# Two transformer blocks on one core: bias tables by a single fp32 product, and another order of the first loads

## What is computed

```python
h = rmsnorm(x, norm_mix[0])
b_gate, c_gate, u = jnp.split(h @ w_in, 3, axis=-1)
```

```python
bucket = t5_bucket(k_pos[None, :] - q_pos[:, None])
bias = rel_bias[bucket].astype(jnp.float32).transpose(2, 0, 1)
s = jnp.einsum('bhcqd,bhcsd->bhcqs', qblk, kt).astype(jnp.float32) * scale + bias[None, :, None]
```

## Time and profile before

| what | value |
|---|---|
| median of 3 runs | 1266.78 us (1266.71 to 1266.91) |
| the profiled execution | 1267.27 us |
| its span | 1265.4 us |
| TensorE busy | 1239.2 us, 98% of the span |
| VectorE, ScalarE, POOL busy | 79%, 67%, 3% |
| instructions | 18129 |
| DMA, moved in all | 325.22 MB, mean 257 GB/s |

### The profile page before, as it was taken

One profiled execution on the slowest core, in us unless ns is written; L12 is line 12 of the kernel. 1 busy time (PEld: TensorE's weight loads), 2 busy tenths in 40 slices (PEclk: granted clock), 3 DMA queues, 4 the chain that ended last, 5 costly groups with the idle time before them and its releaser, 6 DMA issues.

```text
span 1265.4 us, 18129 instructions
## 1 busy us (share of the span) xinstructions
PE 1239.2 (98%) x5924; PEld 1017.3 (80%) x5924; DVE 1001.6 (79%) x1397; ACT 844.1 (67%) x1218; POOL 39.1 (3%) x47
## 2 busy tenths in 40 slices
PE   7999999999999999999999999999999999999998
PEld 6888888888778787888788888888786877888887
DVE  6577555556977899999999999999999887765664
ACT  5666444446755788888888878888887587544442
POOL 0000000000100000000000000000100121000000
PEclk9999999999999999999999999999999999999999
DMA  9735555554233699999999999999996633455540
GB/s 356 275 133 215 190 193 175 190 199 166 68 133 134 252 379 373 378 348 365 368 379 360 353 360 379 375 356 366 376 422 264 238 146 115 163 176 195 178 155 34
DMA packets 48197, 325.22 MB, mean 257 GB/s; under 512 B 5417, under 2 KB 6705, under 8 KB 9873
## 3 DMA queue, kind: packets, MB, share of 16 engines
q1 hardware_dynamic: 44704, 316.40, 66.3%
q10 hardware_dynamic: 2752, 5.77, 1.2%
q0 software_dynamic: 688, 2.36, 0.5%
HBM read 318.74 MB, written 5.77 MB: 256 GB/s over the span
## 4 chain that ended last, share of the span: by engine, by line
PE 91%; DVE 4%; ACT 2%; issue 1%; DMA 0%; POOL 0%; SPq 0%; DVEq 0%; ACTq 0%
PE bank L431 26%; PE bank L433 25%; PE bank L432 25%; PE bank L1138 4%; PE bank L1139 2%; PE bank L495 2%; PE bank L845 1%; ACT wh L1196 1%; DVE wl L1827 1%; PE bank L467 1%; PE bank L700 1%; PE bank L1137 1%; PE bank L699 1%; DMA x<-x_dram 0%; DVE xt L1847 0%
## 5 line engine op out<-in xcount | busy, mean ns | idle before, releaser
L1827 DVE TENSOR_TENSOR wl<-raw,wh 128x1024 fp32r<-128x1024 f32 x598 | 714.7, 1219 | 178.0 <-ACT wh L1196 168.9
L1196 ACT ACTIVATE wh<-raw 128x1024 fp32r<-128x1024 f32 x598 | 630.6, 1058 | 273.1 <-PE bank L433 234.2
L431 PE MATMUL bank<-wh,xt 128*128 128x512 f32 (+2 forms) x1026 | 407.5, 397 | 5.7 <-DVE xt L1847 2.5
L433 PE MATMUL bank<-wh,xt 128*128 128x512 f32 (+2 forms) x1026 | 398.1, 388 | 0.0
L432 PE MATMUL bank<-wl,xt 128*128 128x512 f32 (+2 forms) x1026 | 397.5, 387 | 0.0
L431 PEld LDWEIGHTS bank<-wh,xt 128*128 128x128 f32 x1026 | 193.8, 189 | 44.3 <-DVE xt L1847 3.2
L433 PEld LDWEIGHTS bank<-wh,xt 128*128 128x128 f32 x1026 | 193.5, 189 | 40.6
L432 PEld LDWEIGHTS bank<-wl,xt 128*128 128x128 f32 x1026 | 194.1, 189 | 36.3
L431 PE MATMUL bank<-wh,hth 128*128 128x512 f32 x472 | 186.0, 394 | 1.1 <-DVE htl L1895 0.4
L433 PE MATMUL bank<-wh,htl 128*128 128x512 f32 x472 | 184.2, 390 | 0.0
L432 PE MATMUL bank<-wl,hth 128*128 128x512 f32 x472 | 183.8, 389 | 0.0
(11 more groups left out here) (304 smaller groups left out, 815.3 us busy)
## 6 DMA issues: line engine op xcount, KB each, us to landing
raw<-weights_dram SPq DMA_DIRECT2D x299, 1024.0 KB, 5.0
expert_results<-wide ACTq DMA_DIRECT2D x7, 512.0 KB
x<-x_dram SPq DMA_DIRECT2D x2, 512.0 KB, 7.7
wide<-bias_scratch ACTq DMA_DIRECT2D x8, 128.0 KB, 6.8
out_dram<-x SPq DMA_DIRECT2D x4, 256.0 KB, 2.0
fixed<-fixed_dram SPq DMA_DIRECT2D x1, 536.0 KB, 11.7
bias_scratch<-act ACTq DMA_DIRECT2D x2, 256.0 KB, 8.4
bias_scratch<-hbuf ACTq DMA_DIRECT2D x2, 256.0 KB, 15.1
```

Source lines behind the costliest of these rows:

```text
L431: mm(o, lh, wh[:, wi, sl], start=start, stop=False)
L433: return mm(o, ll, wh[:, wi, sl], start=False, stop=stop)
L1196: A(wh[:, c % SPLIT, 0:n], raw[:, (c // 2) % RAW, (c % 2) * UNIT:(c % 2) * UNIT + n], ACT.Copy).then_inc(hi_done, 1)
L1827: V.tensor_tensor(wl[:, c % SPLIT, 0:n], raw[:, (c // 2) % RAW, (c % 2) * UNIT:(c % 2) * UNIT + n], f32(wh[:, c % SPLIT, 0:n]), ALU.subtra ...
```

## The change

The four tables' eight products, two casts, one subtraction and four copies give way to one fp32 product with the bucket table (32 x 4) as its stationary side and the one-hot matrix as its moving side. It writes four rows of 512. It stands behind the third unit of the first chunk. One copy takes the four rows out, and one store on ScalarE's queue writes each of them 128 times.

The identity moves from `fixed` to the head of `cols`. SP's first loads become: columns with identity, first half of x, unit 0, second half of x, unit 1, panel 1, then the bucket table, the one-hot matrix, panel 2, `fixed`, and panels 3 to 5. POOL's two loads wait for unit 1.

```diff
         @block.sync
+            sp.dma_start(cols[:, :], cols_in).then_inc(sem("cols_in"), 16)
+            sp.dma_start(x[:, :, 0:WIDE], halves[:, :, 0:WIDE]).then_inc(sem("x_in0"), 16)
+            sp.dma_start(raw[:, 0, 0:UNIT], weights[0][:, 0:UNIT]).then_inc(sem("first_in"), 16)
+            sp.dma_start(x[:, :, WIDE:D], halves[:, :, WIDE:D]).then_inc(sem("x_in1"), 16)
+            sp.dma_start(raw[:, 0, UNIT:2 * UNIT], weights[0][:, UNIT:2 * UNIT]).then_inc(raw_full[0], 16)
+            sp.dma_start(raw[:, 1, :], weights[1]).then_inc(raw_full[1], 16)
             sp.dma_start(relb[:, :], relb_in).then_inc(sem("rel_in"), 16)
             sp.dma_start(onehot, onehot_in).then_inc(sem("rel_in"), 16)
-            sp.dma_start(fixed[:, 0:P], fixed_in[:, 0:P]).then_inc(sem("cols_in"), 16)
-            sp.dma_start(cols[:, :], cols_in).then_inc(sem("cols_in"), 16)
-            sp.dma_start(x[:, :, 0:WIDE], halves[:, :, 0:WIDE]).then_inc(sem("x_in0"), 16)
-            sp.dma_start(raw[:, 0, :], weights[0]).then_inc(raw_full[0], 16)
-            sp.dma_start(x[:, :, WIDE:D], halves[:, :, WIDE:D]).then_inc(sem("x_in1"), 16)
-            sp.dma_start(raw[:, 1, :], weights[1]).then_inc(raw_full[1], 16)
-            sp.dma_start(fixed[:, P:NFIXED], fixed_in[:, P:NFIXED]).then_inc(sem("fixed_in"), 16)
-            for p in range(2, RAW):
+            sp.dma_start(raw[:, 2, :], weights[2]).then_inc(raw_full[2], 16)
+            sp.dma_start(fixed[:, :], fixed_in).then_inc(sem("fixed_in"), 16)
+            for p in range(3, RAW):
...
         @block.gpsimd
+            g.memset(half[:, :], -0.5).then_inc(sem("half"), 1)
+            pool.wait_ge(sem("half"), 1)
+            pool.wait_ge(raw_full[0], 16)
             pool.dma_start(rows[:, :], rows_in.to_broadcast((P, NROWS))).then_inc(sem("pos_in"), 16)
             pool.dma_start(posi[:, :], pos_in).then_inc(sem("pos_in"), 16)
...
         @block.tensor
-            rel_bias(0)
-            rel_bias(1)
-            pe.wait_ge(sem("cols_in"), 32)
+            def rel_bias():
+
+                pe.wait_ge(sem("rel_in"), 32)
+                mm(bank[4][0:NB2, :], relb[:, :], onehot, start=True, stop=True).then_inc(sem("rel_T"), 1)
+
+            pe.wait_ge(sem("cols_in"), 16)
             turn_half("mix0", 0, 4)
-            rel_bias(2)
-            rel_bias(3)
             turn_half("mix0", 1, 6)
...
-                chunk512(U_IN + 4 * j, 0, bank[2 * (j % 3):2 * (j % 3) + 2], normed("mix0") if j == 0 else None)
+                chunk512(U_IN + 4 * j, 0, bank[2 * (j % 3):2 * (j % 3) + 2], normed("mix0") if j == 0 else None,
+                         {2: rel_bias} if j == 0 else {})
...
         @block.scalar
-            for h in range(NB2):
-                sc.wait_ge(sem("rel_c"), h + 1)
-                sc.dma_start(scratch[h * P:(h + 1) * P, :], rel_rows[h]).then_inc(sem("rel_st"), 16)
+            sc.wait_ge(sem("rel_c"), 1)
+            sc.dma_start(scratch[0:NB2 * P, :].rearrange("(h p) n -> h p n", p=P),
+                         rel_rows[:, None, :].to_broadcast((NB2, P, WIDE))).then_inc(sem("rel_st"), 16)
...
             for c in range(4, SPLIT):
                 split_lo(c, 0)
+            dv.wait_ge(sem("rel_T"), 1)
+            V.tensor_copy(rel_rows, bank[4][0:NB2, :]).then_inc(sem("rel_c"), 1)
```

More of the change, by code:

```diff
@@ L90 @@
 _at = 0
-for _name, _n in (("mix0", 8), ("ffn0", 8), ("mix1", 8), ("ffn1", 8), ("attn2", 8), ("mlp2", 8), ("qa", 3), ("kva", 2),
+for _name, _n in (("ident", P), ("mix0", 8), ("ffn0", 8), ("mix1", 8), ("ffn1", 8), ("attn2", 8), ("mlp2", 8), ("qa", 3), ("kva", 2),
                   ("qn", 1), ("kn", 1), ("conv", 24), ("bq", 1), ("bk", 1), ("sub", 1), ("router", 64)):
@@ L105 @@
 _at = 0
-for _name, _n in (("ident", 128), ("mask", 384), ("ctab", 128), ("stab", 128), ("freq", 32), ("iota", 8),
+for _name, _n in (("mask", 384), ("ctab", 128), ("stab", 128), ("freq", 32), ("iota", 8),
                   ("before", 128), ("slots", 128), ("every", 128), ("fold", 8)):
@@ L189, in build @@
         by_expert = results[0:(NE - 1) * P, :].rearrange("(e p) n -> e p n", p=P)
-        ident = fixed[:, FIXED["ident"]:FIXED["ident"] + P]
+        ident = cols[:, COLS["ident"]:COLS["ident"] + P]
         maskt = fixed[:, FIXED["mask"]:FIXED["mask"] + 384]
         onehot = ebuf[0:BUCKETS, 0, :]
-        picked = hth[0:BUCKETS, 0:2, :]
-        relh, rell = (v[0:BUCKETS, 2:4, :].rearrange("p a (h n) -> p (a h) n", h=2) for v in (hth, htl))
-        rel_rows = (act[:, 0, 3072:3584], act[:, 1, 3072:3584], hbuf[:, 0, :], hbuf[:, 1, :])
+        rel_rows = act[0:NB2, 0, 3072:3584]
         NORMS = ("mix0", "ffn0", "mix1", "ffn1", "attn2", "mlp2")
@@ L313, in _ @@
         def _(sp):
+            halves = x_in.rearrange("(t p) d -> p t d", p=P)
+            sp.dma_start(cols[:, :], cols_in).then_inc(sem("cols_in"), 16)
[4 more added lines that the diff above has]
+            sp.dma_start(raw[:, 1, :], weights[1]).then_inc(raw_full[1], 16)
             sp.dma_start(relb[:, :], relb_in).then_inc(sem("rel_in"), 16)
             sp.dma_start(onehot, onehot_in).then_inc(sem("rel_in"), 16)
-            sp.dma_start(fixed[:, 0:P], fixed_in[:, 0:P]).then_inc(sem("cols_in"), 16)
-            sp.dma_start(cols[:, :], cols_in).then_inc(sem("cols_in"), 16)
-            halves = x_in.rearrange("(t p) d -> p t d", p=P)
-            sp.dma_start(x[:, :, 0:WIDE], halves[:, :, 0:WIDE]).then_inc(sem("x_in0"), 16)
-            sp.dma_start(raw[:, 0, :], weights[0]).then_inc(raw_full[0], 16)
-            sp.dma_start(x[:, :, WIDE:D], halves[:, :, WIDE:D]).then_inc(sem("x_in1"), 16)
-            sp.dma_start(raw[:, 1, :], weights[1]).then_inc(raw_full[1], 16)
-            sp.dma_start(fixed[:, P:NFIXED], fixed_in[:, P:NFIXED]).then_inc(sem("fixed_in"), 16)
-            for p in range(2, RAW):
+            sp.dma_start(raw[:, 2, :], weights[2]).then_inc(raw_full[2], 16)
+            sp.dma_start(fixed[:, :], fixed_in).then_inc(sem("fixed_in"), 16)
+            for p in range(3, RAW):
                 sp.dma_start(raw[:, p, :], weights[p]).then_inc(raw_full[p], 16)
@@ L351, in _ @@
             g = nc.gpsimd
+            g.memset(half[:, :], -0.5).then_inc(sem("half"), 1)
+            pool.wait_ge(sem("half"), 1)
+            pool.wait_ge(raw_full[0], 16)
             pool.dma_start(rows[:, :], rows_in.to_broadcast((P, NROWS))).then_inc(sem("pos_in"), 16)
             pool.dma_start(posi[:, :], pos_in).then_inc(sem("pos_in"), 16)
-            g.memset(half[:, :], -0.5).then_inc(sem("half"), 1)
-            pool.wait_ge(sem("half"), 1)
             def rsqrt(tag, a, b, n):
@@ L620, in _ @@
             for j in range(6):
-                if j < 2:
-                    pe.wait_ge(sem("rel_c"), 2 * j + 2)
+                if j == 2:
+                    pe.wait_ge(sem("rel_c"), 1)
                 if j >= 3:
                     pe.wait_ge(sem("in_c"), 2 * (j - 2))
-                chunk512(U_IN + 4 * j, 0, bank[2 * (j % 3):2 * (j % 3) + 2], normed("mix0") if j == 0 else None)
+                chunk512(U_IN + 4 * j, 0, bank[2 * (j % 3):2 * (j % 3) + 2], normed("mix0") if j == 0 else None,
+                         {2: rel_bias} if j == 0 else {})
                 if j == 3:
@@ L1190, in split_hi @@
             def split_hi(c, i):
-                sc.wait_ge(raw_full[(c // 2) % RAW], 16 * (c // ROUND + 1) + 16 * i)
+                if isinstance(i, int) and c + ROUND * i == 0:
+                    sc.wait_ge(sem("first_in"), 16)
+                else:
+                    sc.wait_ge(raw_full[(c // 2) % RAW], 16 * (c // ROUND + 1) + 16 * i)
                 if c >= SPLIT:
@@ L1311, in _ @@
             A(stat[:, 0:1], half[:, 0:1], ACT.Copy)
-            sc.wait_ge(sem("cols_in"), 32)
+            sc.wait_ge(sem("cols_in"), 16)
             for c in range(4):
@@ L1623, in _ @@
             squares("attn2", 1)
-            sc.wait_ge(sem("rel_st"), 16 * NB2)
+            sc.wait_ge(sem("rel_st"), 16)
             for h in range(NB2):
@@ L1969, in rotate @@
                 link(V.tensor_tensor(upper, t3, t4, ALU.add))
[L1972 to L1985, removed]
+            dv.wait_ge(sem("cols_in"), 16)
             for c in range(4):
@@ L2099, in _ @@
             dv.wait_ge(sem("norm_rs"), nth("ffn0") + 1)
-            dv.wait_ge(sem("rel_st"), 16 * NB2)
+            dv.wait_ge(sem("rel_st"), 16)
             ffn("ff", U_FF1, FF1 // FG, 2, 4, FG, 2, 0, leave=leave_ff1)
@@ L2872 @@
     cols = np.concatenate([
-        column(w["norm_mix"][0]), column(w["norm_ffn"][0]), column(w["norm_mix"][1]), column(w["norm_ffn"][1]),
+        np.eye(P, dtype=np.float32), column(w["norm_mix"][0]), column(w["norm_ffn"][0]), column(w["norm_mix"][1]), column(w["norm_ffn"][1]),
         column(w["attn_norm_g_2"][0]), column(w["mlp_norm_g_2"][0]), column(w["mla_q_a_norm"][0]),
```

8 lines of the change are left out of this document (removed).

## The result

The changed kernel takes **1279.76 us** (median of 4 runs, 1278.07 to 1280.71) against 1266.85 us for the kernel before, timed beside it (4 runs, 1266.71 to 1268.15). The ratio is 1.0103 with a 95% interval of 1.0090 to 1.0116: 12.9 us slower. The profiled execution took 1279.76 us, span 1278.0.

The account below looks back on a forecast made before the run. TensorE, busy 98%, was taken as the bound. Unit 6 at 10.6 + 36 x 0.2268 + 2.1 + 1.1 + 9.22 = 31.2 us against 32.86, 1.7 us earlier, took 1266.78 to 1265.1 us; range 1263.5 to 1267.4.

Parts of the forecast that it names:

- Part 4: Product, copy, angles, sine, issue and split ahead of unit 6: 9.22 us against 8.17 covered, TensorE waits 1.05 us.
- Part 5: Position load, fixed tables and table store cost nothing; positions land at 18.7 us, fixed tables near 18.
- The fourth rival: Four-partition table store, at an assumed sixteenth of 405 GB/s, clogs weight loads from 22.9 us: 1272 us; chance 0.04.
- Part 1: First loads reordered: x's halves land at 5.65 and 8.25 us, products start at 10.6 us, 4.0 earlier.
- Part 2: TensorE's low clock at the start of the products costs 2.1 us, against 1.9 before.
- Part 3: The one new fp32 product, behind unit 2 on TensorE's path, takes 1.1 us.
- the first rival: Angles' chain hides within units 3 to 5, the 1.05 us wait goes: 1263.4 to 1264.1 us; chance 0.24.
- The third rival: Position load lands late, at 26.7 us, and VectorE's wait delays unit 6: 1269.0 us; chance 0.06.

Follow-up runs that it names:

- e1: Changed kernel with the small zero-row store issued ahead of the table store on ScalarE's queue; 1266.71 us, ratio 0.9999 to the kernel before.
- e3: Changed kernel with the table store's source spread over all 128 partitions, each storing its row four times; 1264.84 us, ratio 0.9994 to the kernel before.
- e2: Changed kernel with the table store cut into four, one row from one partition each; 1273.22 us, ratio 1.0041 to the kernel before.
- e4: As e1, but with the load order of the kernel before the change; 1268.66 us, ratio 1.0015 to the kernel before.
- e5: As e3, with the copy behind the angle tables and the store behind the splits of units 6 to 9; 1266.55 us, ratio 1.0001.
- e7: Changed kernel with half the table store at its place, the other half behind the third group of units' splits; 1267.18 us, ratio 0.9999.
- e8: Changed kernel with the four source rows on partitions 0, 4, 8, 12; 1272.60 us, ratio 1.0046 to the kernel before.
- e9: Changed kernel with the four source rows on partitions 0, 32, 64, 96; 1275.97 us, ratio 1.0073 to the kernel before.
- e6: Changed kernel with the table store as two half-width stores, same bytes in twice the packets; 1292.13 us, ratio 1.0202 to the kernel before.

## Why the prediction was wrong

The forecast was 1265.1 us, no change. The sign came from one line.

**The step that failed** is in Part 4, "the sine, one DMA issue and the high part of unit 6", with the issue taken at 1.28 us as in the earlier trace rows, together with Part 5, which put the table store "at no cost". Part 5 asked of the store only when its data would be wanted, at 112.60 us. It did not ask what stands behind the store on its own queue. The next issue there was in the sum, at a price measured behind another store: before, the tables went out in four stores and the issue behind them took 1.28. Behind one store with 128 packets on each of four engines it measured 12.68. e1 takes that and nothing else away and the loss goes; e3 does the same by spreading the source.

**The fourth rival** had the store, the sign and roughly the size (1272), but another mechanism. In the changed kernel the weights were not clogged: from 27 to 32 us they still moved 1.79 MB. When unit 6 was wanted its weights were long in place, and only the engine that splits them stood still. The mechanism that the rival describes exists, and e2 shows it; it takes all 16 engines on one partition at a time, not four on four. Its assumed "sixteenth of 405 GB/s", 25, is what was measured.

**Part 1, the loads: right in kind, smaller.** The first transposes start at 5.19 (forecast 5.5 to 6.2), the products at about 11.2 (second product 11.63 less one slow pitch of 0.43; forecast 10.6). The second half of x was late: 7.2 us after its issue, near 9.4, where 8.25 was forecast. e4 puts the load order at 2.4 us, where 4.0 of earlier start less 0.2 for the clock had been forecast.

**Part 2, the clock: the price moves.** In the changed kernel the pitch fell near 13.5 us, 2.3 after the products began: 2.3 x 0.47 = 1.1 us lost for the 2.1 forecast. In e1, the same instructions up to there, it fell near 15.3, 3.9 after the start (second product 11.81 less 0.43), as it did before (3.84): 1.8 us. In e1's timeline the step is this:

```profile
14.80 0.63 PE L433 MATMUL bank<-wh,xt 128*128 128x512 f32 x1
15.23 0.53 PE L431 MATMUL bank<-wh,xt 128*128 128x512 f32 x1
15.60 0.39 PE L432 MATMUL bank<-wl,xt 128*128 128x512 f32 x1
15.82 0.39 PE L433 MATMUL bank<-wh,xt 128*128 128x512 f32 x1
```

**Part 3, the product: right.** Two instructions, 20.61 to 21.55, 0.94 us for 1.1. The four passes of the Trainium skill ("FP8 and Floating Point Precision", TensorE Precision Notes) gave an estimated 0.85; the row lies between.

**Part 4, the rest of the chain: right.** With an issue of 1.28 in place of 12.68 unit 6 would have been ready at 42.00 - 11.40 = 30.6 us (forecast 31.2), and e3 measures the wait as 0.61 (forecast 1.05). In e1, with the zero row's issue out of the chain, TensorE doesn't wait at all: the first rival, "the chain hides", has the mechanism right as soon as that one issue is elsewhere, though not its time (1263.4 to 1264.1, where e1 took 1266.71).

**Part 5, the landings: right.** The positions landed at about 12.1 + 6.9 = 19.0 us (forecast 18.7), the fixed tables at 5.8 + 12.5 = 18.3 (forecast 18), and VectorE's cast at 22.27 waited for neither. The third rival falls.

Without the hold the forecast would have held: e1, e3, e5 and e7 measure 0.9994 to 1.0001, all with intervals that take in no change. None of them beats the kernel before by what can be measured, though their starts are 1.4 to 2.1 us ahead at 100 us.

## What to carry to other kernels

A DMA issue is an instruction of its engine: here the split behind one stood idle for 12.47 us. When several small stores are joined into one, ask what is queued behind it on that engine, how many transfers it puts on each DMA engine, and which partitions it reads. Put small issues ahead of large stores, and give a store with a repeated source as many partitions as the source can be had on; four rows in four neighbouring partitions were the slowest of the places tried here (25 GB/s).

## What the runs showed of the hardware

- An issue of 4 KB was held for 12.68 us (after), 8.10 (e8), 8.62 (e9) and 17.60 us (e6), and each time went through with 78 to 94 packets left on each of its engines; e6's second half, 128 packets per engine itself, went through with 75 left. With 64 put there (e7) the 4 KB issue took 0.80. The exact count stays open.
- The same 1 MB moved at 25 GB/s from partitions 0 to 3 through 4 engines, at some 27 through 16 (e2), at a steady 50 from 0, 32, 64, 96 (e9) and at 98 to 102 from 0, 4, 8, 12 (e8). Beside saturated weight loads e8's source gave 26.
- 16 engines on one partition at a time left the weight queue 22 GB/s (e2); four engines on four neighbours left it 346 (e1).
- TensorE's clock rose 2.3 us after the products began in the changed kernel and 3.9 in e1, behind the same transposes and products. Why it differs stays open.
